# When GpSimd sums the squares for the gate's norm, and which half of the tokens opens the second block

## The reference

```python
h = h + jnp.square(jax.nn.relu(m @ w_up[i])) @ w_down[i]
gate = jax.nn.sigmoid(rmsnorm(h, norm_ple[i]) @ w_ple_gate[i])      # 1024 x 1024
h = h + gate * (p[i] @ w_ple_proj[i])                               # 256 x 1024
...
return rmsnorm(h, norm_final)                                       # end of block 1
...
h = jnp.concatenate([meta, x], axis=1)                              # 16 tokens in front
u = rms_norm(h, ln_w[l])
... = jnp.split(u @ w_in[l], IN_OFFSETS, axis=-1)
```

## Time and profile before

| | us |
|---|---|
| median of the runs | 1931.04 |
| profiled execution, its time | 1931.94 |
| profiled execution, its span | 1930.1 |
| TensorE busy in the span | 1860.0 (96%) |
| VectorE, ScalarE, GpSimd busy | 1185.2, 784.4, 551.8 |
| granted TensorE clock, mean | 0.986 |

### The profile page before, as it was taken

How to read it: one execution, slowest core, us unless ns; L and a number is a source line. 1 busy time by engine, 2 the same in 40 slices (tenths; PEclk the granted TensorE clock), 3 DMA queues, 4 the chain that set the end, 5 groups by cost and what they waited for, 6 DMA issues and landing times.

```text
span 1930.1 us, 24206 instructions
## 1 busy us (share of the span) xinstructions
PE 1860.0 (96%) x9462; PEld 1511.5 (78%) x9462; DVE 1185.2 (61%) x1805; ACT 784.4 (41%) x1404; POOL 551.8 (29%) x554
## 2 busy tenths in 40 slices
PE   8999999899988999999999999989999999899999
PEld 5788788666777888887888887869988897676787
DVE  6678545555787666676877886455344348466642
ACT  6765223455543333333333354452211136455520
POOL 0120026440637565610000033550522234011100
PEclk9999999999999999999999999999999999899999
DMA  4143433300314444479555401113101314311131
GB/s 160 45 149 103 148 89 105 110 30 26 133 68 157 166 141 160 152 294 394 180 200 193 175 1 43 33 59 133 43 23 44 110 57 145 110 34 34 44 131 66
DMA packets 110026, 216.27 MB, mean 112 GB/s; under 512 B 37512, under 2 KB 42888, under 8 KB 105816
## 3 DMA queue, kind: packets, MB, share of 16 engines
q1 hardware_dynamic: 109624, 214.49, 32.7%
q10 hardware_dynamic: 288, 0.22, 0.0%
HBM read 153.82 MB, written 60.87 MB: 111 GB/s over the span
## 4 chain that ended last, share of the span: by engine, by line
PE 76%; DVE 10%; ACT 6%; POOL 4%; issue 3%; DMA 1%; SPq 0%; DVEq 0%; POOLq 0%; ACTq 0%
PE ps L361 10%; PE ps L362 10%; PE ps L363 10%; PE ps L2326 5%; PE ps L1948 5%; PE ps L2328 5%; PE ps L2327 5%; PE ps L1950 5%; PE ps L1949 5%; PE ps L3642 4%; PE ps L378 3%; PE ps L706 2%; ACT sc L1502 1%; PE ps L3543 1%; PE ps L3631 1%
## 5 line engine op out<-in xcount | busy, mean ns | idle before, releaser
L361 PE MATMUL ps<-xh,whi 128*128 128x512 f32 (+2 forms) x1160 | 457.7, 395 | 9.8 <-DVE wlo L330 5.5
L362 PE MATMUL ps<-xl,whi 128*128 128x512 f32 (+2 forms) x1160 | 442.2, 381 | 0.0
L363 PE MATMUL ps<-xh,wlo 128*128 128x512 f32 (+2 forms) x1160 | 441.8, 381 | 0.0
L361 PEld LDWEIGHTS ps<-xh,whi 128*128 128x128 f32 x1160 | 219.9, 190 | 58.7 <-issue 10.7
L363 PEld LDWEIGHTS ps<-xh,wlo 128*128 128x128 f32 x1160 | 219.5, 189 | 39.9
L362 PEld LDWEIGHTS ps<-xl,whi 128*128 128x128 f32 x1160 | 220.0, 190 | 33.1
L1948 PE MATMUL ps<-oph,wsh 128*128 128x512 f32 x448 | 176.1, 393 | 11.8 <-DVE stu L2062 5.8
L2326 PE MATMUL ps<-dnh_b,dnh_a 128*128 128x512 f32 x448 | 175.5, 392 | 4.6 <-DVE dn_b L2352 4.4
L1949 PE MATMUL ps<-opl,wsh 128*128 128x512 f32 x448 | 175.3, 391 | 0.0
L1950 PE MATMUL ps<-oph,wsl 128*128 128x512 f32 x448 | 175.2, 391 | 0.0
L2327 PE MATMUL ps<-dn_b,dnh_a 128*128 128x512 f32 x448 | 175.1, 391 | 0.0
(11 more groups left out here) (515 smaller groups left out, 3402.9 us busy)
## 6 DMA issues: line engine op xcount, KB each, us to landing
wraw<-panels SPq DMA_DIRECT2D x70, 512.0 KB, 3.6
dnr_b<-ff_d SPq DMA_DIRECT2D x28, 1024.0 KB, 8.0
dnr_a<-down SPq DMA_DIRECT2D x28, 1024.0 KB, 5.1
ff_d<-st SPq DMA_DIRECT2D x64, 256.0 KB, 5.8
ff_d<-stt SPq DMA_DIRECT2D x48, 256.0 KB, 6.0
upx<-up SPq DMA_DIRECT2D x16, 512.0 KB, 3.8
upy<-up SPq DMA_DIRECT2D x16, 512.0 KB, 5.5
hT<-x SPq DMA_DIRECT2D x8, 512.0 KB, 4.9
```

The lines of the kernel that those rows point to most:

```text
L361: pe.matmul(out, h, xh[:, xk, c0:c1_], start=(n == 0), stop=False)
L362: pe.matmul(out, h, xl[:, xk, c0:c1_], start=False, stop=False)
L363: mm = pe.matmul(out, l, xh[:, xk, c0:c1_], start=False, stop=(n == nk - 1))
```

## The change

It does four things.

1. GpSimd's additions 8 to 15 for the gate's norm wait until VectorE has made the last `xl` of the gate's input. ScalarE makes squares 4 to 7 earlier (in the last step but one of the MLP), 8 to 10 ahead of the last four `xh`, and 11 to 15 behind them. The common term of the last quarter is added a step earlier. The third `sqh` buffer moves off the bytes of `praw`, a weight buffer, and with it goes a wait of SyncE ahead of the weight loads.
2. TensorE's two small steps for the norm's factor move back by 12 matmuls each: `sums_pe` from the middle of gate 1's first half to its end, `factors_pe` from the middle of gate 1's second half to its end.
3. Panel gate 7 is worked with the second half of the tokens first, and so is the first panel of the second block. `next_input` follows: all of c0 = 512, then c0 = 0. VectorE finishes proj 7's second half first, and its first half after `next_input((0, 1), 0)`.
4. The split of the second block's second panel moves on ScalarE ahead of the last four output squares, and on VectorE ahead of the 16 leading tokens.

```diff
-    sqh = [M(f"sqh{i}", 96 + 2 * i, [512]) for i in range(3)]
+    sqh = [M("sqh0", 96, [512]), M("sqh1", 98, [512]), at("sqh2", c_at + 4096, [512])]
...
             if s == step_of[g, 3]:
+                for k in range(4, 8):
+                    h_square_act(act, w, k)
                 w.wait_ge(*pe_ml.at("down", g, 7, 3))
...
         gate_high(act, w, range(4), 512)
-        for k in range(4, 12):
+        for k in range(8, 11):
             h_square_act(act, w, k)
         gate_high(act, w, range(4, 8), 0)
-        for k in range(12, 16):
+        for k in range(11, 16):
             h_square_act(act, w, k)
...
-            if g == last and i in (5, 7):
+            if g == last and i in (5, 7, 3):
                 for n in range(4):
-                    common_added(dve, w, 22 if i == 5 else 12, n)
+                    common_added(dve, w, {5: 22, 7: 12, 3: 21}[i], n)
...
     def down_pool(pool, w):
         for k in range(16):
+            if k == 8:
+                w.wait_ge(*dve_pl.at("low", 7, 0))
             h_square_pool(pool, w, k)
...
-        return HALVES[::-1] if n == 0 else HALVES
+        return HALVES[::-1] if n in (0, 7) else HALVES
...
-            gate(n, each([[(0,)], [], [(1,)]] if n == 1 else [], norm))
+            gate(n, each([[], [(0,)], [], [(1,)]] if n == 1 else [], norm))
...
-        next_input((0,), 0)
-        sigmoid(7, 512)
-        next_input(range(1, 8), 0)
         next_input(range(8), 512)
+        sigmoid(7, 0)
+        w.wait_ge(*pe_pl.at("gate", 7, 0))
+        next_input(range(8), 0)
+        act_split(act, w, IN20 + 1)
         output_squares_act(act, w, 7)
...
         gate(7)
+        project(7, (512,))
+        next_input(range(8), 512)
+        gate_tile(7, 0)
+        next_input((0, 1), 0)
         project(7, (0,))
-        gate_tile(7, 512)
-        next_input((0, 1), 0)
-        project(7, (512,))
         next_input(range(2, 8), 0)
-        next_input(range(8), 512)
+        dve_split(dve, w, IN20 + 1)
...
+            cols = cols2(kind)[::-1] if n == 0 else cols2(kind)
+            pe_dense(pe, w, pe_i2, (kind, j), IN20 + n, dve_i2, XX2, u2, cols=cols, behind=behind)
...
-        w.wait_ge(*pool_pl.at("sum", 15))
         sp_weights(sp, w, IN20 + 2)
```

More of the change, by code:

```diff
@@ L2491, in down_dve @@
         gate_low(dve, w, range(2), 512)
-        common_added(dve, w, 21, 0)
         down_read(dve, w, NS - 1, 0)
@@ L2495, in down_dve @@
         dve_split(dve, w, PLE0)
-        common_added(dve, w, 21, 1)
         down_read(dve, w, NS - 1, 1)
@@ L2499, in down_dve @@
         for n in (2, 3):
-            common_added(dve, w, 21, n)
             down_read(dve, w, NS - 1, n)
@@ L2621, in gate @@
                     split_p_act(act, w, k)
+                root_act(act, w, pe_pl, act_pl, "ple")
                 act_split(act, w, proj_panel(0))
-                root_act(act, w, pe_pl, act_pl, "ple")
                 factors_act(act, w, pe_pl, act_pl, "ple")
-            for c0 in [c for c, _ in gate_cols(n)] if n < 7 else (0,):
+            for c0 in [c for c, _ in gate_cols(n)] if n < 7 else (512,):
                 sigmoid(n, c0)
@@ L2672, in gate @@
                     split_p_dve(dve, w, k)
+                root_dve(dve, w, act_pl, dve_pl, "ple")
                 dve_split(dve, w, proj_panel(0))
-                root_dve(dve, w, act_pl, dve_pl, "ple")
                 w.wait_ge(*pe_pl.at("sums", "ple"))
-            for c0 in [c for c, _ in gate_cols(n)] if n < 7 else (0,):
+            for c0 in [c for c, _ in gate_cols(n)] if n < 7 else (512,):
                 gate_tile(n, c0)
@@ L3000, in project2_pe @@
             behind = each([[], [("sums",)], [("norms",)], []] if n == 1 else [], lambda part: final_stats_pe(pe, w, part))
-            pe_dense(pe, w, pe_i2, (kind, j), IN20 + n, dve_i2, XX2, u2, cols=cols2(kind), behind=behind)
+            cols = cols2(kind)[::-1] if n == 0 else cols2(kind)
+            pe_dense(pe, w, pe_i2, (kind, j), IN20 + n, dve_i2, XX2, u2, cols=cols, behind=behind)
             for m in turn_behind.get(n, ()):
@@ L3018, in project2_act @@
         for n, (kind, j) in enumerate(rows):
-            act_split(act, w, IN20 + n + 1)
+            if n:
+                act_split(act, w, IN20 + n + 1)
             if n == 1:
@@ L3047, in project2_dve @@
         for n, (kind, j) in enumerate(rows):
-            dve_split(dve, w, IN20 + n + 1)
             if n == 0:
                 continue
+            dve_split(dve, w, IN20 + n + 1)
             before = [f2_left(n)[0].at(*f2_left(n)[1])] if n >= 3 else []
```

## The result

The changed kernel took 1937.37 us (median of six, 1937.17 to 1938.09), the kernel before 1930.82 in the same comparison (six, 1929.75 to 1931.47): ratio 1.0034, 95% interval 1.0024 to 1.0044, +6.5 us. The forecast was 1935.7 and its whole range 1932.6 to 1938.2: the measured time lies inside that range, 1.7 above the forecast and 0.2 above the forecast's own narrower range (1934.0 to 1937.2). The profiled execution took 1938.04 with a span of 1936.2, against a span of 1930.1 before.

The account below looks back on a forecast made before the run. TensorE's stands were taken as the bound: 3.62 us ahead of gate 0, 1.69 and 1.06 at the second block's input. Terms +0.4 and +4.3 make +4.7 on the 1931.04 median: 1935.7 us, range 1932.6 to 1938.2.

Parts of the forecast that it names:

- both stands: TensorE waits forecast ahead of gate 1 (2.9 us) and ahead of the second block's first panel (6.7 us).
- the two terms of the forecast: Gate's input, +0.4 us, and second block's input, +4.3 us.
- Gate 0 at the MLP's end, at full clock: Gate 0 starts at 1160.9 instead of 1164.49, without the low clock, and ends at 1172.1.
- Additions 8 to 12 hold gate 1: GpSimd's late additions delay square 15 and gate 1's split; gate 1 starts at 1175.0 (1174.4 to 1175.6).
- Who waits at the split: At gate 1's split VectorE and GpSimd lock each other out; gate 1 starts between 1174.4 and 1175.7, rather later.
- The factors, then gate 2 at +7.05: Factors come 13.1 us after gate 1's start, at 1188.1; gate 2 follows 7.05 later, at 1195.2.
- the first part: The gate's input, gates 0 to 2: +0.4 us, from -1.2 to +2.4, with 1.0 taken for the clock.
- The bank of proj 7: Second block's first panel waits for bank 0's late read: 6.7 us stand, 2.3 of low clock, +4.3 in all.
- Each step keeps its distance: From the final sums on, every step keeps its distance to TensorE, so the +4.3 us loss stays.
- The first part loses by itself: Rival at the gate's input: full 2.4 us clock drop and another 1 behind the factors; +7.1, 1938.1; 13%.
- the bank is free in time: Rival at the second block's input: first group doesn't wait for the multiplication; second part -2.6, whole -2.2, 1928.8; 6%.
- gate 1's split is in time: Rival at gate 1: additions let ScalarE through early, gate 1 starts at 1172.1; whole +0.8, 1931.8; 4%.

Follow-up runs that it names:

- run 6: The changed kernel without the line that makes GpSimd's addition 8 wait for the last low part: 1933.91 us.
- run 4: The changed kernel with ScalarE's split of panel gate 1 ahead of squares 11 to 15: 1934.34 us.
- run 7: The changed kernel with proj 7's second half first, gate 1's ScalarE split ahead of squares 11 to 15, and the norm's factors 12 matmuls earlier: 1924.98 us.
- run 3: The kernel before with only the changes to gate 7 and the second block's input: 1934.05 us.
- run 1: The changed kernel with TensorE's halves of panel proj 7 exchanged, second half first: 1931.86 us.
- run 8: run 7's kernel with gate 7's first-half tile and proj 7's first half earlier in VectorE's order: 1926.52 us.
- run 9: The changed kernel with squares 8 to 15 taken in turn from the two token halves: 1935.99 us.
- run 5: The changed kernel with proj 7's second half first and ScalarE's gate 1 split ahead of squares 11 to 15: 1928.95 us.

## Why the prediction was right, step by step

The direction and both stands came as forecast, for the reasons given. How near the number came is in part luck: the two terms of the forecast came to +2.2 and +4.0 in the profile for +0.4 and +4.3, and three further differences that it didn't name (-0.8, -0.8, +1.6) cancel there.

VectorE's timeline of the changed kernel at this place, then ScalarE's (they answer to the earlier trace rows):

```profile
1149.96 4.52 DVE L1931 SCALAR_TENSOR_TENSOR xl<-hT,vec,xh 128x512 fp32r<-128x512 f32 x6
...
1156.34 1.21 DVE L330 TENSOR_TENSOR wlo<-wraw,whi 128x1024 fp32r<-128x1024 f32 x1
...
1161.91 2.73 DVE L1931 SCALAR_TENSOR_TENSOR xl<-hT,vec,xh 128x512 fp32r<-128x512 f32 x4
...
1173.20 2.25 DVE L330 TENSOR_TENSOR wlo<-wraw,whi 128x1024 fp32r<-128x1024 f32 x1 [8.48 <-ACT whi L318]
```

```profile
1171.59 0.63 ACT L2420 ACTIVATE sqh<-hT 128x512 f32<-128x512 f32 x1 [0.60 <-POOL acch L1742]
1172.13 1.04 ACT L318 ACTIVATE whi<-wraw 128x1024 fp32r<-128x1024 f32 x1
```

- **Gate 0 at the MLP's end, at full clock.** Right: 1160.04, no stand, and its split done at 1157.55 for the 1158 said. The wait on GpSimd had no part in it: without it, in run 6, gate 0 starts without a stand too.
- **Additions 8 to 12 hold gate 1.** Right in mechanism, each size too small, and gate 1's start lies 0.9 us beyond the bounds given for it. Counted from gate 0's start, gate 1 was put at +14.1 us (1175.0 - 1160.9), and came at +15.56. The first addition came at +4.68 for +4.2: six `xl` took 4.5 us, 0.75 each and not 0.67. The five additions lasted 6.84 us (1164.72 to 1171.56), not 6.4 with the signal: the 1.26 was read from a row in which I had not asked whether one addition waits for the other. The split on VectorE took 2.25, near the upper end of the bounds and not the middle. These three make about 1.3 of the 1.5.
- **Who waits at the split.** The 1.08 us an `xl` of the earlier trace rows was the mean of two kinds: in the kernel before the first three of the six start 0.66 apart, before GpSimd begins, and the last two 1.70 apart, beside additions that are 1.70 apart as well. The split lasted 2.25 us where it began beside GpSimd's additions. In run 4 the same split began 0.09 us ahead of GpSimd's first two additions (1166.10 and 1166.19): it took 1.22, and the two additions together 3.73 for the 2.7 that two take elsewhere. So the loser pays about 1 us, whichever engine it is. This is what the page cited in the prediction (the Trainium skill, SBUF — State Buffer, Who interferes with whom) states, and the later end for which it spoke is what came.
- **The factors, then gate 2 at +7.05.** The distance was exact: 1197.20 - 1190.15 = 7.05, and it is 7.05 in thirteen of the fourteen profiles, wherever the factors stand (7.50 in run 7, where matmuls ran slow). The clock, taken at 1.0, cost 1.45 (gate 1 to the factors took 14.55 for 13.1). In all the first part came to +2.2 us, not +0.4: this is the term that was mis-sized, by 1.5 for gate 1's start and 0.45 for the clock; it still lies inside the bounds given for the part, -1.2 to +2.4, because the clock didn't cost its full 2.4. One reading in it was wrong in kind: I opened with the 2.4 us of low clock in gate 0 as a cost, and run 3 shows that they cost nothing.
- **The bank of proj 7.** Right: 6.7 us predicted, 6.70 measured; run 1 takes it away by the order of the two halves alone. The clock cost a little less than the 2.3 taken (slow matmuls to 1298.17), and from gate 7's start to the final sums the change is 37.01 for 33.00 us, +4.0 where +4.3 was said. Each step of the chain to the multiplication came within 0.1 us of the row that it was taken from.
- **"Each step keeps its distance" behind the sums.** Wrong in this profile by +1.6: 25.51 for 23.92 us. Against it stands -0.8 between gates 2 and 7 (78.88 for 79.69 us): the stand of 2.27 at 1271.19 brought the lower level before and did not after, at 1272.60.
- **The rivals.** None came true whole. "The first part loses by itself" had the right sign and size for the whole (1938.1), but by a fall of 2.4 and another behind the factors, which did not come. Two workings in this list don't hold, and no chance hung on them. The time of "the bank is free in time" uses 1300.2 for the next panel, where 1286.9 + 11.2 + 1.2 gives 1299.3. And "gate 1's split is in time" needs additions under (1172.1 - 2.7 - 1165.1) / 5 = 0.86 us, not 0.7; none took so little.

By stretches: -0.8 ahead of all, +2.2 to gate 2, -0.8 to gate 7, +4.0 to the sums, +1.6 to `f`: +6.2, as the marks at 1332.40 and 1338.60 say.

## What to carry to other kernels

When an instruction is held back to keep an engine free, list what is queued behind whoever waits for it: here a wait on GpSimd held a square on ScalarE, and behind the square a weight split that TensorE needed. It cost 3.6 us in the changed kernel and bought nothing; with the split moved ahead of the squares it cost nothing that could be told. When the order of the halves is turned in one stage, turn it in the stage that frees its banks too; a bank ring passes a late read on as a stand of full size (6.7 us), and one reversed loop took 5.1 of the stretch back. Before a slow stretch is counted as a cost, ask what is late next if it is fast.

## What the runs showed of the hardware

- A GpSimd addition of 128x512 that waits for the semaphore of the one before starts 1.43 us behind it, one that doesn't 1.25; both last 1.28 to 1.30.
- Beside each other the two engines go in step: `xl` start 0.66 us apart alone and 1.70 beside GpSimd's additions, and the additions are then 1.70 apart too (the kernel before from 1153.32, run 8 from 1289.01). A mean over a row can hide this, as the 1.08 of the earlier trace rows did.
- A stand of the same length does not always bring the lower level (1.2 GHz). Behind the 3.62 us ahead of gate 0 the granted clock fell in one profile and held in another; behind 2.27 us at proj 6 it fell in six of the fourteen profiles and held in eight; behind 2.12 us in run 6 it held; behind 3.35 in run 9 the first matmuls still ran at 0.39 to 0.40 us and those of 0.63 began 1.5 us after the restart; behind 4.26 to 4.29 us ahead of gate 1 it fell in all five profiles; behind each of the six stands of 6.5 us or more the first matmul already lasted 0.79 to 0.80. TensorE had been busy at full level ahead of all of them. A term for the clock is thus a chance times 1.5 to 2.4 us, except for stands as long as the last two kinds.
- It also fell without a long stand. Behind the norm's sums (16 matmuls of 128x1) with 0.56 to 0.57 us ahead of them it fell in runs 4, 7 and 8 and held in run 5, and behind the final sums (32 such matmuls), with no stand ahead of or behind them, it fell in all fourteen profiles.
- The marks ahead of the changed stretch moved by up to 3.5 us from one execution to the next; what moves them is not shown. The granted clock alone is not it: between 535 and 560 it was 1.00 in the profile before and 0.95 in the changed kernel's, but the stand ahead of the same matmul was 2.73 us and 1.15, and it started at 539.61 and 539.97. The lower level took the place of most of the stand.
